# Seven-product down blocks interleaved with the gate and up units, two of four weight sums per set made by adding transfers that GpSimd issues

## The reference, cut to what matters

```python
S, D_MODEL = 512, 2048
D_FF = 5632
def swiglu(h, wg, wu, wd):
    return (jax.nn.silu(h @ wg) * (h @ wu)) @ wd

h = rms_norm(x, norm_mix_g[i])
x = x + nsa_mixer(h, ...)
h = rms_norm(x, norm_ffn_g[i])
x = x + swiglu(h, ffn_w_gate[i], ffn_w_up[i], ffn_w_down[i])
```

## Time and profile before

| | us |
|---|---|
| median of 3 runs | 2402.48 (2402.32 to 2403.24) |
| profiled execution, its own time | 2402.24 |
| its span, first to last instruction | 2400.3 |
| TensorE busy (PE) | 2314.3, 96% |
| VectorE busy (DVE) | 1374.2, 57% |
| ScalarE busy (ACT) | 777.4, 32% |
| GpSimd busy (POOL) | 38.6, 2% |
| DMA | 219.48 MB, mean 91 GB/s |

### The profile page before, as it was taken

The page is one execution under the profiler, slowest core; times in us unless marked ns, Lnnn a source line. Parts: engine busy times, 40 slices in busy tenths (PEclk is TensorE's granted clock), DMA queues, the critical chain, the costliest instruction groups (busy, mean ns, idle before and its releaser), DMA issues.

```text
span 2400.3 us, 32032 instructions
## 1 busy us (share of the span) xinstructions
PE 2314.3 (96%) x12083; PEld 1974.1 (82%) x12083; DVE 1374.2 (57%) x2028; ACT 777.4 (32%) x1147; POOL 38.6 (2%) x44
## 2 busy tenths in 40 slices
PE   6999999999999999999999999999999999999997
PEld 6898888888889899887878787878787787878786
DVE  5333566665665556455564738383746555564747
ACT  4332344443443334322322323232322322222322
POOL 1000000000010000000000000000000000000000
PEclk9999999999999999999999999999999999999998
DMA  5343211212213222233232423323232323242313
GB/s 172 113 114 88 71 54 46 71 53 55 60 64 132 66 68 76 85 122 111 77 121 80 123 88 105 97 89 106 79 119 76 114 89 113 71 128 82 114 62 105
DMA packets 212943, 219.48 MB, mean 91 GB/s; under 512 B 12780, under 2 KB 186881, under 8 KB 211505
## 3 DMA queue, kind: packets, MB, share of 16 engines
q1 hardware_dynamic: 211856, 211.86, 28.8%
q0 software_dynamic: 928, 5.44, 0.7%
HBM read 213.05 MB, written 4.19 MB: 91 GB/s over the span
## 4 chain that ended last, share of the span: by engine, by line
PE 85%; DVE 9%; issue 3%; ACT 2%; DMA 1%; SPq 0%; DVEq 0%; POOL 0%; ACTq 0%
PE ps L1196 83%; DVE down L1102 2%; DVE x_rows L1131 2%; DVE wl L708 1%; PE ps L1490 1%; DMA down<-in_ffn_w_down_dram 1%; ACT wh L424 1%; DVE t L1102 1%; DMA x_rows<-in_x_dram 0%; DVE ffn_work L1154 0%; DVE ffn_work L1151 0%; PE ps L1482 0%; DVE x_rows L724 0%; DVE nmax L973 0%; PE ps L1526 0%
## 5 line engine op out<-in xcount | busy, mean ns | idle before, releaser
L1196 PE MATMUL ps<-hTh,wh 128*128 128x512 f32 (+1 forms) x1968 | 767.6, 390 | 6.7 <-DVE wl L708 3.5
L1196 PE MATMUL ps<-hTh,wl 128*128 128x512 f32 (+1 forms) x1968 | 760.8, 387 | 0.0
L1196 PE MATMUL ps<-hTl,wh 128*128 128x512 f32 (+1 forms) x1968 | 759.9, 386 | 0.0
L708 DVE TENSOR_TENSOR wl<-raw,wh 128x1024 fp32r<-128x1024 f32 x298 | 363.5, 1223 | 533.6 <-ACT wh L424 532.4
L424 ACT ACTIVATE wh<-raw 128x1024 fp32r<-128x1024 f32 x298 | 314.5, 1059 | 634.3 <-PE ps L1196 525.4
L1196 PEld LDWEIGHTS ps<-hTh,wh 128*128 128x128 f32 x1968 | 371.1, 189 | 79.9 <-issue 3.9
L1196 PEld LDWEIGHTS ps<-hTh,wl 128*128 128x128 f32 x1968 | 370.3, 188 | 75.3
L1196 PEld LDWEIGHTS ps<-hTl,wh 128*128 128x128 f32 x1968 | 370.8, 188 | 72.0 <-issue 0.2
L1196 PE MATMUL ps<-wh,opsh 128*128 128x512 f32 x616 | 244.7, 397 | 40.9 <-DVE x_rows L1131 34.1
L1196 PE MATMUL ps<-wl,opsh 128*128 128x512 f32 x616 | 242.3, 393 | 0.0
L1196 PE MATMUL ps<-wh,opsl 128*128 128x512 f32 x616 | 242.0, 393 | 0.0
(11 more groups left out here) (174 smaller groups left out, 2074.6 us busy)
## 6 DMA issues: line engine op xcount, KB each, us to landing
raw<-in_ffn_w_gate_dram SPq DMA_DIRECT2D x176, 256.0 KB, 3.0
raw<-in_ffn_w_up_dram SPq DMA_DIRECT2D x176, 256.0 KB, 3.0
down<-in_ffn_w_down_dram SPq DMA_DIRECT2D x176, 256.0 KB, 3.3
raw<-in_nsa_w_in_dram SPq DMA_DIRECT2D x164, 256.0 KB, 3.0
raw<-in_nsa_w_out_dram SPq DMA_DIRECT2D x64, 256.0 KB, 3.2
x_rows<-in_x_dram SPq DMA_DIRECT2D x4, 1024.0 KB, 12.7
raw<-in_nsa_cmp_w_dram SPq DMA_DIRECT2D x16, 256.0 KB, 3.0
x_rows<-in_x_dram POOLq DMA_DIRECT2D x4, 1024.0 KB, 5.8
```

The source lines that it names most:

```text
L708: nc.vector.tensor_tensor(dst, src, hi.bitcast(f32), ALU.subtract).then_inc(done, 1)
L1196: return nc.tensor.matmul(out_, a, b, start=start, stop=stop, skip_group_check=True)
```

## The change

1. `MIXED` becomes g0, g1, d0, d1, then six times a gate or up unit followed by two products (g2, d2, d3, g3, d4, d5, and so on to g7, d12, d13), then g8 to g15.
2. T1 and T3 are no longer made on VectorE. The block `down[1]` is loaded a second time, into `t3` (two more transfers of 256 KB per set), and GpSimd issues two transfers per set that add while they write: `down[1] += down[0]` (T1) once both blocks are loaded, and `t3 += down[3]` (T3). ScalarE and VectorE wait on `t1_summed` and `t3_summed`. T2 and T4 stay on VectorE.
3. VectorE takes a product's result out (`down_out`) at the start of its position, ahead of any work on operands there.
4. The left operands from g0 to g7 are split after d13 instead of after g7, since the products that read the old ones now run to that place. The third and fourth of the four differences and sums move in between the operand splits, and d0, d1 and d2 each wait for the operands that they read (`m_lo`), where d0 waited for all.

```diff
--- before.py
+++ after.py
@@ -35,13 +35,15 @@
 TURN = G_UNITS + DOWN
 
 UPS = [("g", j) for j in range(G_UNITS)]
-MIXED = UPS[:2] + [("d", j) for j in range(14)] + UPS[2:]
+MIXED = [("g", 0), ("g", 1), ("d", 0), ("d", 1)] \
+    + [e for r in range(6) for e in (("g", 2 + r), ("d", 2 + 2 * r), ("d", 3 + 2 * r))] + UPS[8:]
 DOWNS = [("d", j) for j in range(DOWN)]
 PAIRS = (SLABS - 3) // 2
 
-T3_DONE, T1_DONE, T2_DONE, T4_DONE = 1, 2, 3, 4
+T2_DONE, T4_DONE = 1, 2
 S1, S2, S3, N4, M0A, M1A, M1B = range(7)
 LEFT = [M0A, M1A, S2, S1, S3, N4, M1B]
+W12_COPY = 4
 LAST = GROUPS - 1
 OWN = LAST * REP
 
@@ -186,6 +188,7 @@
         r2_den, r2_root, r2_diag, rb_done = sem("r2_den"), sem("r2_root"), sem("r2_diag"), sem("rb_done")
         gs_ready, silu_done, m_ready, m_hi, m_lo = (sem(n) for n in ("gs_ready", "silu_done", "m_ready", "m_hi", "m_lo"))
         down_loaded = [sem(f"down_loaded{i}") for i in range(4)]
+        t3_loaded, t3_summed, t1_summed = sem("t3_loaded"), sem("t3_summed"), sem("t1_summed")
         sums_ready, m_sums = sem("sums_ready"), sem("m_sums")
         y_added, stored = sem("y_added"), sem("stored")
 
@@ -249,7 +252,9 @@
 
         def operands_at(order, j):
 
-            return ("g", j)
+            if order is DOWNS or order is UPS or j == G_UNITS - 1:
+                return ("g", j)
+            return ("d", DOWN - 1)
 
         block = ctx.enter_context(nc.Block())
 
@@ -320,10 +325,12 @@
 
             def down_block(r, s, i, quad):
 
+                dst, done = (t3[:, :], t3_loaded) if r == W12_COPY else (down[:, r, :], down_loaded[r])
+                r = 1 if r == W12_COPY else r
                 c, col = r // 2, quad * 1024 + r % 2 * 512
                 for b in range(2):
                     src = w_down_v[c][:, bass.ds(i * 2 + s, 1), b, col:col + 512].rearrange("p s n -> p (s n)")
-                    sp.dma_start(down[:, r, b * 512:(b + 1) * 512], src).then_inc(down_loaded[r], 16)
+                    sp.dma_start(dst[:, b * 512:(b + 1) * 512], src).then_inc(done, 16)
 
             def ffn_loads(order, n0, s, i):
 
@@ -334,13 +341,13 @@
                             up_unit(F0 + j, s + (j + RAW) // G_UNITS, i, (j + RAW) % G_UNITS)
                         if ("d", 0) not in order and j == 12:
                             sp.wait_ge(rb_done, 1)
-                            for r in (0, 2, 1, 3):
+                            for r in (0, 1, 3, W12_COPY, 2):
                                 down_block(r, 0, 0, 0)
                         continue
                     quad, o = j // QUAD, j % QUAD
-                    if o in (2, 3, 5, 6) and (s < SLABS or quad == 0):
+                    if o >= 2 and (s < SLABS or quad == 0):
                         wait(sp, lo_ready, n0 + p + 1, 2 * TURN, i)
-                        down_block({2: 0, 3: 1, 5: 3, 6: 2}[o], s - 1 + quad, i, 1 - quad)
+                        down_block({2: 0, 3: 1, 4: W12_COPY, 5: 3, 6: 2}[o], s - 1 + quad, i, 1 - quad)
 
             for j in range(RAW):
                 sp.wait_ge(lo_ready, F0 + j - RAW + 1)
@@ -416,6 +423,14 @@
             pool.dma_start(gain_row[:, :], ffn_g.to_broadcast([P, D])).then_inc(gain2_loaded, 16)
             pool.wait_ge(r2_den, 1)
             inverse_root(rr[:, :], r2_root)
+
+            for turn in range(2 * SLABS):
+                pool.wait_ge(down_loaded[0], 32 * (turn + 1))
+                pool.wait_ge(down_loaded[1], 32 * (turn + 1))
+                pool.dma_start(down[:, 1, :], down[:, 0, :], accum_op=ALU.add).then_inc(t1_summed, 16)
+                pool.wait_ge(down_loaded[3], 32 * (turn + 1))
+                pool.wait_ge(t3_loaded, 32 * (turn + 1))
+                pool.dma_start(t3[:, :], down[:, 3, :], accum_op=ALU.add).then_inc(t3_summed, 16)
 
 
         @block.scalar
@@ -661,10 +676,12 @@
                     r = (0, 2, 0, 0, 0, 3)[o]
                     wait(act, down_loaded[r], 32 * (turn + 1), 128, i)
                     src = down[:, r, :]
+                elif o in (3, 4):
+                    src, done = ((down[:, 1, :], t1_summed), (t3[:, :], t3_summed))[o - 3]
+                    wait(act, done, 16 * (turn + 1), 64, i)
                 else:
-                    src, done = {2: (down[:, 0, :], T2_DONE), 3: (down[:, 1, :], T1_DONE), 4: (t3[:, :], T3_DONE),
-                                 6: (down[:, 2, :], T4_DONE)}[o]
-                    wait(act, sums_ready, 4 * turn + done, 16, i)
+                    src, done = (down[:, 0, :], T2_DONE) if o == 2 else (down[:, 2, :], T4_DONE)
+                    wait(act, sums_ready, 2 * turn + done, 8, i)
                 wait(act, units_used, n - RING + 1, 2 * TURN, i)
                 copy(wh[:, n % RING, :], src).then_inc(hi_ready, 1)
 
@@ -1105,18 +1122,14 @@
 
                 turn, o = 2 * (s - 1) + j // QUAD, j % QUAD
                 if o == 2:
-                    wait(dve, sums_ready, 4 * turn + T1_DONE, 16, i)
+                    wait(dve, lo_ready, n, 2 * TURN, i)
+                    wait(dve, t1_summed, 16 * (turn + 1), 64, i)
                     add(down[:, 0, :], down[:, 1, :], down[:, 3, :])
-                    wait(dve, sums_ready, 4 * turn + T2_DONE, 16, i)
+                    wait(dve, sums_ready, 2 * turn + T2_DONE, 8, i)
                     add(down[:, 2, :], down[:, 0, :], down[:, 2, :])
                 src = (down[:, 0, :], down[:, 2, :], down[:, 0, :], down[:, 1, :], t3[:, :], down[:, 3, :], down[:, 2, :])[o]
                 wait(dve, hi_ready, n + 1, 2 * TURN, i)
                 lo(wl[:, n % RING, :], src, wh[:, n % RING, :], lo_ready)
-                if o == 1:
-                    wait(dve, down_loaded[1], 32 * (turn + 1), 128, i)
-                    wait(dve, down_loaded[3], 32 * (turn + 1), 128, i)
-                    add(t3[:, :], down[:, 1, :], down[:, 3, :])
-                    add(down[:, 1, :], down[:, 0, :], down[:, 1, :])
 
             def down_out(n, s, i, j):
 
@@ -1136,6 +1149,8 @@
                 both = rbc[:, :].rearrange("p (a c) -> p a c", a=1).to_broadcast([P, 2, S])
                 for p, (kind, j) in enumerate(order):
                     n, b = n0 + p, j // 8
+                    if kind == "d":
+                        down_out(n, s, i, j)
                     if s == 0 and j == 1:
                         hidden_part(3)
                     if s == 0 and j == 4:
@@ -1158,23 +1173,23 @@
                         s1, s2, s3, n4 = (ffn_work[:, c, a:a + 256] for c in range(2) for a in (0, 256))
                         own.done(nc.vector.tensor_tensor(s1, m0b, m1b, ALU.subtract))
                         nc.vector.tensor_tensor(s3, m0a, m0b, ALU.subtract)
-                        own.settle()
-                        own.done(nc.vector.tensor_tensor(s2, s1, m0a, ALU.subtract))
-                        own.settle()
-                        nc.vector.tensor_tensor(n4, m1a, s2, ALU.add).then_inc(m_sums, 1)
                     for b in range(2):
                         if (kind, j) == operands_at(order, 8 * b + 7):
+                            m0a, m1a = ffn_work[:, 2, 0:256], ffn_work[:, 3, 0:256]
+                            s1, s2, n4 = ffn_work[:, 0, 0:256], ffn_work[:, 0, 256:512], ffn_work[:, 1, 256:512]
                             wait(dve, m_hi, 6 * s + 3 * b + 1, 12, i)
-                            lo(opsl[:, b, M0A, :], ffn_work[:, 2, 0:256], opsh[:, b, M0A, :], m_lo)
+                            lo(opsl[:, b, M0A, :], m0a, opsh[:, b, M0A, :], m_lo)
+                            own.settle()
+                            own.done(nc.vector.tensor_tensor(s2, s1, m0a, ALU.subtract))
                             wait(dve, m_hi, 6 * s + 3 * b + 2, 12, i)
                             lo(opsl[:, b, M1A:M1B + 1, :].rearrange("p o c -> p (o c)"), ffn_work[:, 3, :],
                                opsh[:, b, M1A:M1B + 1, :].rearrange("p o c -> p (o c)"), m_lo)
+                            own.settle()
+                            nc.vector.tensor_tensor(n4, m1a, s2, ALU.add).then_inc(m_sums, 1)
                             wait(dve, m_hi, 6 * s + 3 * b + 3, 12, i)
                             lo(opsl[:, b, S1:N4 + 1, :].rearrange("p o c -> p (o c)"),
                                ffn_work[:, 0:2, :].rearrange("p a c -> p (a c)"),
                                opsh[:, b, S1:N4 + 1, :].rearrange("p o c -> p (o c)"), m_lo)
-                    if kind == "d":
-                        down_out(n, s, i, j)
                     if p + RING < len(ahead):
                         turn, (what, unit) = ahead[p + RING]
                         (up_split if what == "g" else down_split)(n + RING, turn, i, unit)
@@ -1576,8 +1591,8 @@
                     n = n0 + p
                     wait(pe, lo_ready, n + 1, 2 * TURN, i)
                     if kind == "d":
-                        if j == 0:
-                            wait(pe, m_lo, 6 * s, 12, i)
+                        if j < 3:
+                            wait(pe, m_lo, 6 * s - 2 + j, 12, i)
```

## The result

The changed kernel takes **2412.89 us** (median of 6 runs, 2411.38 to 2415.10) against 2402.86 us of the kernel before in the same comparison (6 runs, 2401.43 to 2404.03): ratio 1.0043, 95% interval 1.0032 to 1.0053. It is slower by 10 us, which is more than the 0.2% that can be told apart, and outside the range of 2388 to 2409 us. The profiled execution took 2415.10 us itself; its span is 2412.6 us against 2400.3 before, 12.3 us more.

The account below looks back on a forecast made before the run. The prediction took TensorE, busy 96% of the span, as the bound. Slabs -10 us, clock falls +13 and the last slab -5.8 summed to -2.8, so 2399.5 us against 2402.24, range 2388 to 2409 us.

Parts of the forecast that it names:

- The waits at d7 and d8 of the slabs: TensorE's two waits per slab for results from VectorE would both go: -3.9 us a slab.
- The new wait at g8: In each slab g8 would wait 2.6 us for the last results, costing +2.9 us with handing over and restart.
- The adding transfers: GpSimd's T1 and T3 transfers would land within bounds of 3.3 and 11.2 us; cost taken as 0.
- d0 of the last slab: d0 would start 3.8 us after g15 in place of 6.6: -2.8 us, with one 3.4 us clock fall.
- the sentence on the extra traffic: Additional loads of 512 KB a set: no raw block used less than 8 us after it can land, cost 0.
- Rival 3: Added traffic delays raw loads so gate and up units wait: one us a slab, +10, 2409.5 us; chance 0.05.
- the number of falls: Clock falls of 3.41 us behind g8's wait in eight of ten slabs, 1.65 us each: +13 us, bounds 0 and +17.
- the middle of the last slab: One wait of 1.3 us plus restart in place of 1.50 and 1.67 with theirs: -2.1 us.
- the last slab: All terms of the last slab, from d0's shorter wait to its middle, together: -5.8 us.

Follow-up runs that it names:

- e2: Changed kernel with all four sums back on VectorE and no adding transfers, so the new order alone: 2402.84 us.
- e4: Changed kernel, but GpSimd issues T3's adding transfer of the next slab's first set only after g11's low part: 2402.68 us.
- e3: Changed kernel with the old order of units (all 14 products behind g1), keeping the adding transfers: 2390.56 us.
- e1: Changed kernel, but g8 waits for 13 of the 14 results and g9 for all 14: 2363.97 us.
- e7: Changed kernel with all four sums on VectorE, no adding transfer, and g8 waiting for 13 of the 14 results: 2366.11 us.
- e5: Changed kernel with twelve matmuls whose result nobody reads added ahead of g8 in each slab: 2394.35 us.

## Why the prediction was wrong, step by step

**Right.** The waits at d7 and d8 of the slabs went, -3.9 us each. The new wait at g8 is there, and by its own working it was 2.6 us idle: e2 and e4 have 2.55 to 2.56, with 2.71 us from start to start where 2.9 was taken. The adding transfers land in 6.0 us, inside the bounds of 3.3 and 11.2 us. d0 of the last slab is idle for 3.80 us (3.8) with one fall of 3.41 us behind it.

**The step that failed first** is the sentence on the extra traffic, "no raw block is used less than 8 us after it can land: 0". That slack must be meant as the time until TensorE uses the unit, since ScalarE copied raw blocks as they landed even before (32 waits for such loads). What it left out is VectorE's fixed order: a late copy holds up a low part, and the result that stands behind it. In the new order VectorE, done with the operands of g7, runs through g9, d12, g10 and d13 without a pause, and SyncE may issue g10's load only after g8's low part, at 1389.05. VectorE comes to g10's low part at 1396.36, so ScalarE's copy must start by 1395.3, 6.2 us after the issue. A load that lands in 3.3 leaves under 3 us of slack, not 8, and T3's transfer took it and 1.0 us more. Rival 3, with 0.05 of the chances, had the late load and nearly the size, +1 us a slab (the waits grew by 0.8, and the falls came on top). It had the wrong path: gate and up units that wait for loads 8 us late, where it was g8 that waited for d13's result, with loads 3 us late. The adding transfer was costed by how long it takes itself, and not by what it does to others.

**The second** is the number of falls. Eight of ten slabs at 1.65 us made +13; all ten had one, and three were of 6.83 us, +20.5 with what lies inside the waits taken off. Without the collision (e2, e4) it is ten of 3.41 us, +17, which was the upper bound. The 3.41 us at 0.50 that the prediction took for one fall are those of the earlier trace rows, and seven of the ten had them. How often a fall comes was its estimate, from two falls behind the four longest waits before, of 1.80 to 1.90 us. The runs had 20 falls behind 20 waits of 2.55 to 2.56 us (e2, e4) and ten behind ten of 3.2 to 3.6 us in the changed kernel. No wait in the slabs of any run lies between 1.90 and 2.55 us, so from what length on a fall is certain was not shown.

**The third** is the middle of the last slab, "one wait of 1.3 us": there were two, 0.86 and 1.70 us idle.

```profile
2386.84 0.47 PE L1211 MATMUL ps<-wh,opsh 128*128 128x512 f32 x1 [0.86 <-DVE x_rows L1144]
2391.51 0.47 PE L1211 MATMUL ps<-wh,opsh 128*128 128x512 f32 x1 [1.70 <-DVE x_rows L1144]
```

The second is what T2, T4 and a low part cost, and 0.4 us longer than reckoned. The first looks like the collision of e3, with T1's transfer: ScalarE waited 4.26 us for the block of d8. No run takes that transfer alone out of the last slab, so this is argued and not shown. That takes the last slab from -5.8 to -4.6 us.

**The sum with these terms:** -39 + 35.4 + 20.5 - 4.6 = +12.3 us, which is what the spans show; with the terms of e4, whose waits lost 27.2 us and whose falls cost 17, the ten slabs come to +5 and the kernel to +0.6, and e4 measured +0.3 against before.

**What the prediction didn't ask** is whether g8 had to wait for d13 at all. It took the wait as given and costed it, 2.9 us and a fall. e1 shows that it asks for one result too many for the banks it fills. With that mended the change is worth 38 us, and the new order by itself, without any adding transfer, 37 (e7).

## What to carry to other kernels

When an order puts a consumer close behind its producers, read again what each wait asks for: one that was harmless with six units between can ask for more than the buffers need. Put on every load its slack in the new order, from its issue to the step that needs it, and cost an added transfer by what it delays (here 2.8 us on the loads beside it) as well as by its own landing (6.0 us). A standstill of TensorE in the middle of a stream cost its own length here and, at 2.55 us idle and more, about half of the 3.41 or 6.83 us at 0.50 of the clock that came with it; from what length on it does, rows of the kernel at hand must show. In e5 even useless matmuls paid there, 18.5 us.

## What the runs showed of the hardware

- An adding transfer from SBUF to SBUF of 512 KB lands in 6.0 us (median of 44; 4.5 to 8.6). Two loads of 256 KB issued 0.1 to 1.1 us after it landed in 5.8 to 6.5 us in ten slabs, in place of 3.2 to 4.4 (e4), though the DMA engines are 44% busy on average over the slab.
- The clock fell to 0.50 at each of 20 waits of 2.55 to 2.56 us idle (e2, e4) and at each of ten of 3.2 to 3.6 us, behind none of the waits of 0.5 to 0.8 us (e5), and behind none of those at d7 and d8 in the ten slabs of e3, of up to 1.7 us. Before, two waits in 20 of at most 1.90 us had one.
